# Delta rule of a hybrid decoder layer: 32-row diagonal blocks inverted on 128 partitions, decay rows fetched through HBM, solve steps in their old places

## The reference

```python
decay = jnp.exp(jnp.where(ii >= jj, gc[..., :, None] - gc[..., None, :], -jnp.inf))
kb = k * beta[..., None]
a_kk = jnp.where(ii > jj, jnp.einsum('bhnik,bhnjk->bhnij', kb, k) * decay, 0.0)
m = a_kk + jnp.eye(CHUNK, dtype=a_kk.dtype)
rhs = jnp.concatenate([v * beta[..., None], kb * jnp.exp(gc)[..., None]], axis=-1)
sol = lax.linalg.triangular_solve(m, rhs, left_side=True, lower=True, unit_diagonal=True)
...
v_new = u_n - jnp.einsum('bhck,bhkv->bhcv', w_n, state)
o_n = jnp.einsum('bhck,bhkv->bhcv', qd_n, state) + jnp.einsum('bhij,bhjv->bhiv', a_n, v_new)
state = state * cd_n[..., None, None] + jnp.einsum('bhck,bhcv->bhkv', kd_n, v_new)
```

## Time and profile before

| | us |
|---|---|
| median of 3 runs | 1085.33 (1084.62 to 1086.16) |
| profiled execution: span from first to last instruction | 1083.5 |
| PE busy in the span | 1019.8 |
| DVE busy | 303.6 |
| ACT busy | 164.3 |
| POOL busy | 21.3 |

### The profile page before, as it was taken

One profiled execution on the slowest core, in us unless ns is written; L12 is line 12 of the kernel. 1 busy time (PEld: TensorE's weight loads), 2 busy tenths in 40 slices (PEclk: granted clock), 3 DMA queues, 4 the chain that ended last, 5 costly groups with the idle time before them and its releaser, 6 DMA issues.

```text
span 1083.5 us, 12842 instructions
## 1 busy us (share of the span) xinstructions
PE 1019.8 (94%) x5096; PEld 447.5 (41%) x5096; DVE 303.6 (28%) x703; ACT 164.3 (15%) x283; POOL 21.3 (2%) x37
## 2 busy tenths in 40 slices
PE   9999999999999999989999989988999898988898
PEld 7888866333434343434344323232333332223232
DVE  4987754312222222222322111101111111111111
ACT  3513436011111111111001000000111011111101
POOL 3201000000000000000000000000000000000000
PEclk9999999999999999999999999999999999999999
DMA  9724779999999999999999999999999999999997
GB/s 324 283 83 161 279 287 365 405 425 428 425 419 432 434 432 428 432 432 429 428 432 428 427 429 431 431 432 429 431 431 431 431 431 430 431 431 434 425 424 289
DMA packets 39036, 427.64 MB, mean 395 GB/s; under 512 B 8251, under 2 KB 10524, under 8 KB 20188
## 3 DMA queue, kind: packets, MB, share of 16 engines
q1 hardware_dynamic: 37840, 426.84, 93.9%
q10 hardware_dynamic: 1164, 0.34, 0.1%
HBM read 424.42 MB, written 2.75 MB: 394 GB/s over the span
## 4 chain that ended last, share of the span: by engine, by line
PE 50%; DMA 41%; DVE 5%; issue 1%; ACT 1%; SPq 1%; ACTq 0%; DVEq 0%
DMA store<-in_w_gate_up_dram 24%; PE bank L2312 17%; DMA store<-in_w_down_dram 16%; PE bank L2370 13%; PE bank L1789 5%; PE bank L1781 3%; PE bank L2218 2%; PE bank L1916 2%; PE bank L2077 2%; PE bank L2283 1%; DVE flow L1627 1%; PE bank L2335 1%; DVE flow L1620 1%; ACT flow L1010 1%; DVE flow L1625 1%
## 5 line engine op out<-in xcount | busy, mean ns | idle before, releaser
L2312 PE MATMUL bank<-store,flow 128*64 128x512 f32 x2048 | 452.0, 598 | 13.9 <-DMA store<-in_w_gate_up_dram 12.9
L2312 PEld LDWEIGHTS bank<-store,flow 128*64 128x64 f32 x2048 | 145.9, 138 | 314.1 <-issue 289.9
L2370 PE MATMUL bank<-store,flow 128*64 128x512 f32 x992 | 228.1, 610 | 32.1 <-DMA store<-in_w_down_dram 20.5
L1620 DVE TENSOR_SCALAR flow<-bank 128x512 f32<-128x512 f32 x32 | 22.1, 692 | 607.8 <-PE bank L2312 607.8
L2370 PEld LDWEIGHTS bank<-store,flow 128*64 128x64 f32 x992 | 74.0, 140 | 165.5 <-issue 138.4
L1010 ACT ACTIVATE flow<-flow 128x512 f32<-128x512 f32 x32 | 20.2, 630 | 445.0 <-DVE flow L1620 445.0
L2227 PE MATMUL bank<-qkT 64*128 64x512 f32 x248 | 61.9, 616 | 0.0
L1026 ACT COPY qkT<-bank 128x512 f32<-128x512 f32 x31 | 18.2, 586 | 194.6 <-PE bank L2370 194.6
L1020 ACT COPY flow<-flow 128x512 f32 x30 | 33.7, 1124 | 27.5 <-DVE flow L1695 11.2
L2227 PEld LDWEIGHTS bank<-qkT 64*128 64x128 f32 x248 | 21.2, 186 | 40.1 <-issue 40.1
L1781 PE MATMUL bank<-store 128*128 128x256 f32 x160 | 35.5, 381 | 0.0
(11 more groups left out here) (360 smaller groups left out, 671.0 us busy)
## 6 DMA issues: line engine op xcount, KB each, us to landing
store<-in_w_gate_up_dram SPq DMA_DIRECT2D x50, 4096.0 KB, 26.9
store<-in_w_down_dram SPq DMA_DIRECT2D x57, 2048.0 KB, 20.9
store<-in_w_gate_up_dram SPq DMA_DIRECT2D x26, 2048.0 KB, 13.8
store<-in_w_in_dram SPq DMA_DIRECT2D x6, 2048.0 KB, 13.7
store<-in_w_down_dram SPq DMA_DIRECT2D x9, 1024.0 KB, 25.0
store<-in_w_out_dram SPq DMA_DIRECT2D x1, 4096.0 KB, 14.3
store<-in_w_gate_up_dram SPq DMA_DIRECT2D x3, 1024.0 KB, 7.2
flow<-in_w_down_dram SPq DMA_DIRECT2D x1, 2048.0 KB, 11.9
```

The source lines that it names most:

```text
L1620: dve.tensor_scalar(gt, bank[4][:], LIMIT, None, ALU.min).then_inc(g_min, 1)
L2312: ins = mm(dst[SLOTS * hf:SLOTS * (hf + 1), :], rows[:, c:c + SLOTS], store[:, slot_at(j, odd) + c0:slot_at(j, odd) + c0 + 512], start=fir ...
L2370: ins = mm(dst[SLOTS * hf:SLOTS * (hf + 1), :], turned[:, c:c + SLOTS], w[:, hf * 512:(hf + 1) * 512], start=f == 0, stop=f == KT - 1)
```

## The change

- The diagonal blocks grow from 16 to 32 rows (32 blocks in all). They are read back from HBM four times over, on 128 partitions. `J0` inverts the two halves of 16 rows in every copy; a new step `J1` (`join_halves`) picks for each partition a quarter of the columns (a scaling and three multiply-adds over 128 elements, and a copy) and forms the lower left part from two products of 1024 elements, each with a reduce.
- With 32-row blocks the series for the part outside is one power shorter. Stage 7 loses its product into X and ScalarE's copy of it, stage 8 its product N D and the copy into F, and stage `Q` goes. Stages 8 and 9 of tile 1 move from bank 4 to tile 1's own bank.
- The decay rows no longer come from eight scalings and two matmuls. One matmul of 128 columns gives the sums as eight rows; ScalarE copies them, writes them to HBM, reads them back broadcast to all partitions (512 KB) and copies them to banks 0 and 1.
- The first tap of each convolution goes from VectorE to ScalarE (two activations for each `u`). Weight group 3 goes from GpSimd to VectorE and group 4 the other way.
- Steps move: `convolve(1)` ahead of the gates' arithmetic, the sums of x into the wait for ScalarE, `g5` ahead of `01`, the sums of q and `convolve(6)` into the list as `Q0` and `V6` behind `11`, `h5` and `J0` ahead of `u5`, `J1` behind `d4`, and `0E 1E` behind `r2`. ScalarE's evacuation of unit 5 goes behind the exponentials of the decays.

```diff
-FINE = 16
-BLOCKS = 64
+FINE = 32
+HALF = FINE // 2
+BLOCKS = 32
+PARTS = 4
...
-    text = ("01 11 a3 a4 b3 b4 g5 u5 c3 c4 h5 J0 d3 d4 r0 12 e4 02 0E e3 1E r1 a5 r2 n0 17 07 f0 b5 f1 f2 g6 "
-            "08 f3 c5 S0 d5 09 S1 P0 0A P1 e5 S2 h6 T0 0B a6 u6 O0 0Q P2 b6 0C T1 S3 c6 O1 1K T2 d6 P3 0M e6 "
-            "s0 S4 O2 18 P4 0N T3 W0 T4 19 O3 1A 0D O4 S5 P5 1B W1 T5 1Q O5 w0 X0 1C X1 W2 1M A0 1N H0 H1 R0 "
+    text = ("g5 01 11 Q0 V6 a3 a4 b3 b4 h5 J0 c3 c4 u5 d3 d4 J1 r0 12 e4 02 e3 r1 a5 r2 0E 1E n0 17 07 f0 b5 f1 f2 g6 "
+            "08 f3 c5 S0 d5 09 S1 P0 0A P1 e5 S2 h6 T0 0B a6 u6 O0 P2 b6 0C T1 S3 c6 O1 1K T2 d6 P3 0M e6 "
+            "s0 S4 O2 18 P4 0N T3 W0 T4 19 O3 1A 0D O4 S5 P5 1B W1 T5 O5 w0 X0 1C X1 W2 1M A0 1N H0 H1 R0 "
...
-BANK4_STAGES = {2, 8, 9}
+BANK4_STAGES = {(0, 2), (1, 2), (0, 8), (0, 9)}
...
+            first_tap(2)
+
+            sum_rows = arena1[0:T * HG, 1, 0:P]
+            act.wait_ge(gc_psum, 1)
+            st.step(act.copy(sum_rows, bank[3][0:T * HG, 16:16 + P]))
+            act.dma_start(gc_dram, sum_rows).then_inc(ld_small, 16)
             silu(2)
             square(2)
+            act.wait_ge(ld_small, 16 * 9)
+            act.dma_start(arena1[:, 0, :], bass.AP(gc_dram.tensor, 0, [[0, P], [1, T * HG * P]])
+                          ).then_inc(ld_small, 16)
             evac(3)
+            first_tap(3)
...
+            gr = Tally(act, gcrow_ready)
+            act.wait_ge(ld_small, 16 * 10)
+            for t in range(T):
+                gr.mark(act.copy(bank[t][:], arena1[:, 0, 512 * t:512 * (t + 1)]))
...
+                for j in range(1, HALF - 1):
+                    shape = [P, 2, j, HALF - 1 - j]
+                    part = t_new[:, 0:2 * j * (HALF - 1 - j)].rearrange("q (a c r) -> q a c r", a=2, c=j)
+                    st.step(dve.tensor_tensor(part, n_diag[:, :, j + 1:HALF, j].unsqueeze(2).to_broadcast(shape),
+                                              t_of[:, :, 0:j, j].unsqueeze(3).to_broadcast(shape), ALU.mult))
+                    st.step(dve.tensor_tensor(t_of[:, :, 0:j, j + 1:HALF], t_of[:, :, 0:j, j + 1:HALF], part,
+                                              ALU.add))
...
+                st.step(dve.tensor_scalar(picked, columns(0), part_of[:, 0:1], None, ALU.mult))
+                for g in range(1, PARTS):
+                    st.step(dve.scalar_tensor_tensor(out=picked, in0=columns(g), scalar=part_of[:, g:g + 1],
+                                                     in1=picked, op0=ALU.mult, op1=ALU.add))
...
+                st.step(dve.reduce_sum(low_right, product(n_low, first), AX_X))
+                Tally(dve, t_ready).mark(dve.reduce_sum(
+                    own_first[:, :, HALF:], product(t_of[:, 1].rearrange("q k r -> q r k"), low_right), AX_X))
...
                     elif s == 7:
-                        product(X, m["G"], m["L"])
                         ins = product(Y, m["L"], m["G"])
...
                     elif s == 8:
-                        product(Y, m["N"], m["D"])
-                        ins = product(Z, m["G"], m["H"])
+                        ins = product(W, m["G"], m["H"])
...
-                    elif s == "Q":
-                        ins = product(X, m["F"], m["E"])
```

More of the change, by code:

```diff
@@ L91 @@
 ORDER = attention_order()
-PE_STAGES = {1, 2, 7, "K", 8, 9, 10, 11, "Q", 12, 13}
+PE_STAGES = {1, 2, 7, "K", 8, 9, 10, 11, 12, 13}
 DVE_STAGES = PE_STAGES | {"E", "M", "N"}
-ACT_STAGES = {7, "M", "N"}
+ACT_STAGES = {"M", "N"}
 EARLY_STAGES = {1, 2, 7}
-BANK4_STAGES = {2, 8, 9}
-BANK4 = [step for step in ORDER if (step[0] == "gdn" and step[2] in BANK4_STAGES) or step[:2] == ("a", 6)]
+BANK4_STAGES = {(0, 2), (1, 2), (0, 8), (0, 9)}
+BANK4 = [step for step in ORDER if (step[0] == "gdn" and step[1:] in BANK4_STAGES) or step[:2] == ("a", 6)]
 BANK7 = [step for step in ORDER if step[0] in "TO"]
@@ L864, in _ @@
             evac(0)
+            first_tap(1)
             act.wait_ge(dec_dve, 1)
@@ L1202, in _ @@
             convolve(1)
+            dve.wait_ge(ba_psum, 1)
+            dve.wait_ge(ld_small, 16 * 8)
+            ba = bank[3][:, 0:T * 2 * HG].rearrange("p (t n) -> p t n", t=T)
+            st.mark(dve.tensor_scalar(gd[:, 4], ba[:, :, 0:HG], -1.0, None, ALU.mult))
+            dd.mark(dve.tensor_tensor(gd[:, 3], ba[:, :, HG:2 * HG],
+                                      gd[:, 1, 0].unsqueeze(1).to_broadcast([P, T, HG]), ALU.add))
+            dd.mark(dve.tensor_scalar(col[:, 17:18], col[:, 17:18], DH ** -0.5, None, ALU.mult))
+            sums_of_x()
             dve.wait_ge(dec_act, 2)
@@ L1357, in _ @@
                 if kind == "J":
-                    invert_blocks()
+                    (join_halves if a else invert_halves)()
+                    continue
+                if kind == "V":
+                    convolve(a)
+                    continue
+                if kind == "Q":
+                    Tally(dve, q_sums).step(picked_sums(2, gd[:, 9]))
+                    st.step(dve.tensor_scalar(gd[:, 9], gd[:, 9], EPS, EPS * DK * DK, ALU.add, ALU.mult))
                     continue
@@ L1386, in _ @@
                     (X, Y), Z = stage_banks(t, s), bank[4]
+                    W = Y if t else Z
                     if s in PE_STAGES:
@@ L1874, in _ @@
             mm(bank[4][:, 0:8], ucum[:], decays, start=True, stop=True)
+            mm(bank[3][0:T * HG, 16:16 + P], decays, ucum[:], start=True, stop=True)
             Tally(pe, gc_psum).mark(mm(bank[4][:, 8:16], ones[:], decays, start=True, stop=True))
@@ L1890, in _ @@
             l2_sum(1)
-            gr = Tally(pe, gcrow_psum)
-            for t in range(T):
-                pe.wait_ge(ug_ready, HG * (t + 1))
-                gr.mark(mm(bank[t][:], ones[:], ug[:, t, :], start=True, stop=True))
             unit(4)
@@ L2077, in product @@
                             last = mm(dst[:, c], lhsT(h) if callable(lhsT) else lhsT[:, c],
-                                      rhs(h) if callable(rhs) else rhs[:, c], start=start, stop=stop)
+                                      rhs(h) if callable(rhs) else rhs[:, c], start=True, stop=True)
                         return last
```

173 lines of the change are left out of this document (90 added, 83 removed).

## The result

The changed kernel takes 1101.07 us (median of 4 runs, 1100.58 to 1101.54), the kernel before 1085.07 beside it: ratio 1.0145, 95% interval 1.013 to 1.0159. It is 16 us slower. The forecast was 1088.2, with 1083.0 to 1091.8 as its range. The sign was right and the time lies far outside the range.

What follows compares the result with a forecast made beforehand. TensorE's front before the experts was taken as the bound: `f0` 6.1 us late less 3.0 saved behind it, so 3.1 us later, span 1086.6; with the median 1.8 above, 1088.4, named as 1088.2. Range 1083.0 to 1091.8 us.

Steps and rivals of the forecast that it cites:

- What bounds the kernel: TensorE's front up to the experts' start at 183.24 us; a shift of that start passes to the end one for one.
- Rival 3: At the experts: the weight loads absorb the shift of their start, giving 1085.3 us; chance 0.08.
- TensorE's own work: TensorE's front: fewer products and matmuls gain 6.9 us if nothing else waited; `01` starts at 55.8.
- Decay rows: Front, through HBM: write 4.5 us, read 6, copies at 40.3, VectorE's 24 operations end at 47.1; lateness costs 0.
- Rival 2: In the front: the decay rows land late, at 45 us, and cost 3 us more, giving 1091; chance 0.15.
- VectorE's chain: VectorE from the end of `01` through `12`: 25.2 us in all, so `12` has left bank 4 at 88.8.
- `J0`: Inversion step in VectorE's chain: 8.65 us in place of 7.04, bounds 7.5 and 10.
- `J1`: New joining step in VectorE's chain: 6.8 us, bounds 6.3 and 8.
- Bank 4: On TensorE: the turn `02` waits until `12` has left this bank, at 88.8, though TensorE could be there at 84.3.
- rival 1: At the turn `02`: the hand-over of bank 4 doesn't bind, giving 1083.6 us; chance 0.27.
- Behind f0: TensorE from `f0` to the experts: four products, 3.57 us, go; with a wait at `O5` 3.0 us are saved.

Runs made afterwards that it cites:

- experiment 1: The changed kernel with the read-back of the blocks and the write of the inverses each cut into four transfers; 1095.92 us, ratio 1.0092.
- Experiment 8: The changed kernel's front with the old 16-row blocks and solve, Silu of unit 6 moved: decay rows by matmuls 1085.21 us, through HBM 1083.59 us.
- experiment 4: The kernel of experiment 1 with GpSimd's squares waiting until `J1` is done and `r0` moved behind `12`; 1093.96 us, ratio 1.0074.
- experiment 3: The changed kernel with `J1` moved behind `r0`, `12`, `e4` and `02`, its scratch in another buffer; 1100.54 us, ratio 1.0136.
- experiment 2: The changed kernel with idle matmuls, whose result nobody reads, put ahead of `e4`, `02` and `17` on TensorE; 1096.97 us, ratio 1.0104.
- experiment 7: The kernel of experiment 1, Silu of unit 6 moved, inversion left out: 1085.05 us; also with `0E 1E` in their old places: 1082.71 us.
- e10_no_inversion: The kernel of experiment 1 with Silu of unit 6 moved and the inversion left out, so the output is wrong; 1085.05 us, ratio 0.9993.
- e13_no_inversion_early_e: e10_no_inversion with `J1`, only a memset, directly behind `J0` and `0E 1E` in their old places; 1082.71 us, ratio 0.9973.

## Why the prediction was wrong in size

| step | forecast | measured | error |
|---|---|---|---|
| `J0` can start | 70.1 | 74.78 | +4.7 |
| `J0` | 8.65 | 9.24 | +0.6 |
| `u5`, `d3`, `d4` | 1.95 | 1.85 | -0.1 |
| `J1` | 6.8 | 8.5 | +1.7 |
| `02` runs | 88.8 | 95.71 | +6.9 |
| `02` to the end of `a5` | 5.7 | 8.6 | +2.9 |
| from there to `f0` | 5.0 | 5.4 | +0.4 |
| behind `f0` | -3.0 | -1.1 | +1.9 |
| start of the experts | +3.1 | +15.2 | +12.1 |

(No single row explains the 12.1 us: the first four add up to the +6.9 of `02`, and most of the three behind it is the clock. The row from `a5` to `f0` starts at 104.3, where `a5` ended. The last two are against the kernel before, by PE's timelines: from `f0` to the experts 183.16 - 93.37 = 89.8 us there and 198.37 - 109.68 = 88.7 after.)

- **What bounds the kernel** was right. A shift of the experts' start passes to the end one for one, in both directions (+15.2 and +15.4; -3.3 and -3.2). In the other profiles the start and the span agree less closely, by 1.6 us at worst (experiment 1: +10.9 and +12.5), but none shows a shift absorbed. Rival 3 is out.
- **TensorE's own work** was right up to `01`: 56.03 against 55.8.
- **Decay rows** were right. ScalarE's copies ran at 39.85 (forecast 40.3), the 24 operations ended at 46.84 (47.1). ScalarE worked without a pause up to the copies, so the rows had landed within 6.2 us of the read's issue at 33.66; how much sooner isn't seen, and the 40.3 came out without the landing having set it. Rival 2 is out. Experiment 8 puts the gain at 1.6 us.
- **The first step that failed** is the start of `J0` (+4.7 us); the second is the missing clock, below. In "VectorE's chain" the list goes from `h5` straight to `J0`, as if the blocks lay ready. The change reads the blocks back four times over, 512 KB in place of 64, and the prediction has no term for it. By the row used for the decay rows, 3.7 us for 512 KB, it would have landed at 69.7, just in time, which is also what the run with four separate reads showed. What no row of the kernel before held is that the one read in this shape gets a quarter of the engines: 8.74 us. By the Trainium skill (DMA: Bandwidth & Descriptors, Why a DMA increments its semaphore by 16 and not by 1) the number of engines of a transfer is the largest up to 16 that divides the slowest dimension of both its patterns; here these are the four copies of the source and the 128 partitions of the destination, so four. The DMA share of 0.22 to 0.27 agrees.
- **`J0`** lay within its bounds of 7.5 to 10, 0.6 us above the value taken. The copy is not the cause: with its memset it took 0.83 us against 0.54 before, the 0.3 more that was forecast. The 14 pairs took 8.41 us against 6.50, 1.9 more where 1.3 was forecast. Each added element cost about 1.9 ns in the products and 1.2 in the sums, where 1.0 to 1.7 had been estimated, and the steps between the operations cost 0.2 us in all.
- **`J1`** lay above its upper bound of 8. The forecast counted elements and operations, not who else runs: 1.3 us are two operations held up by GpSimd's squares (experiment 4), 0.65 us the second product, of which the 0 to 0.3 us allowed for the reduces pays a part.
- **Bank 4** was the right mechanism, so rival 1 is out. But it is one of two gates on the same chain: experiment 3 opened it and the wait went to `17`.
- **The clock** is the second step that failed: it had no term at all. The prediction made TensorE wait 4.5 us and priced the work behind it at full speed. The wait was 7.8, the clock fell to half, and slow `02`, `e3`, `a5` (2.9 us), the visible part of stage 7 (0.4), `f0` (0.4) and `b5` (0.5) came to about 4.2 us; experiment 2 gave back 4.1. Even the 2.78 us at `17` halve it (experiment 7). But the length of a wait alone doesn't decide: in the change 3.12 us of it stood ahead of `e4`, whose products ran at 1.00. No run here shows what does.
- **Behind f0** four products were to save 3.0 us. Clock apart, they saved 2.0, and in experiment 2, where the clock held, the stretch from `f0` to the experts is 2.0 shorter than before. The wait at `O5` came as forecast (0.77), but another of 0.51 opened at `T3`, where the shorter stage 8 of tile 1 stands just ahead in the list. It was not foreseen. Both gaps are there in experiments 1, 2 and 7 too, and in none of the kernels with the old solve:

```profile
149.12 0.63 PE L2202 MATMUL bank<-ident,store 128*128 128x128 f32 x4 [0.51 <-DVE flow L1549]
...
163.85 0.67 PE L2214 MATMUL bank<-flow,store 128*64 128x128 f32 x8 [0.77 <-ACT flow L1033]
```

The range was too narrow because its bounds were those of the terms in the sum. A DMA and a clock that have no term also have no bounds.

## What to carry to other kernels

Before a chain on one engine is summed, name for each of its steps the transfer that it starts from, with shape, issue and landing; a large broadcast read whose slowest dimension is short is better cut into as many transfers (here 512 KB gained 4.6 us; a write of 128 KB in the same shape gained nothing). A wait of several microseconds on TensorE is to be priced with the possibility that the work behind it starts at half clock: it did behind waits of 2.78, 3.28, 4.59 and 7.76 us, and not behind 1.56, 1.86 and one of 3.12. Work moved from TensorE to VectorE pays only as far as VectorE's part fits beside other TensorE work: here 5.35 us of products were worth 2.0 even with the inversion left out, and the inversion put 17.7 us of VectorE (7.0 before) into the chain that TensorE waits for.

## What the runs showed of the hardware

- 512 KB from HBM in one transfer with an outermost dimension of 4: 8.7 us from issue to landing, 80 to 88 GB/s while it moved. The same bytes in four transfers of 32 partitions: landed within 4.1 us of the first issue.
- A VectorE operation of 128 elements a partition (0.21 to 0.35 us alone) takes 0.88 to 1.03 us when it starts during a GpSimd product of 512, and ends within 0.2 us of that product's end.
- TensorE's granted clock went from 1.00 to 0.50 within the idle 87.95 to 95.7, and was back at 1.00 in the window from 102, 6.3 us after work resumed. After the 2.78 us of idleness at `17` of `e10_no_inversion` it was 0.56 and 0.58 in the windows 92 to 96, and 1.00 from 96 on. After 1.86 us ahead of `f0` in `e13_no_inversion_early_e` it stayed at 1.00.
- A VectorE product of 1024 elements with one factor read transposed: 1.87 us, against 1.22 for one that reads none so; no other run separates the two.
- With twice the elements (28 to 112 in place of 14 to 56, on 128 partitions in place of 64) the inversion's products took about 1.9 ns more for each added element, its sums 1.2.
